# Weight fetches ahead of the modulation pieces, bias rows broadcast in the mixer, one bank waited for per gate product

## What is computed

```python
# first block
mods = silu(c) @ w_ada + b_ada            # 9 pieces of 1024: sh1 sc1 gt1 sh2 sc2 gt2 sh3 sc3 gt3
u = modulate(rmsnorm(h, g_ff1), sh1, sc1)
h = h + 0.5 * gt1 * swiglu(u, w1_gate, w1_up, w1_down)
u = modulate(rmsnorm(h, g_mix), sh2, sc2)
qa, ka, va, xm, o_pre, ga, gb = split(u @ w_in)
ya = diff_attention(qa, ka, va, ...)
xc = silu(causal_conv(xm, conv_w, conv_b))
q, k, v = xc @ w_mq, xc @ w_mk, xm @ w_mv  # per head: the mLSTM's inputs
yb = mlstm(q, k, v, ...)
h = h + gt2 * ((sigmoid(ga) * (ya @ w_proj_a) + sigmoid(gb) * (yb @ w_proj_b)) @ w_out)
u = modulate(rmsnorm(h, g_ff2), sh3, sc3)
h = h + 0.5 * gt3 * swiglu(u, w2_gate, w2_up, w2_down)   # the second feed-forward: "f2"
# second block, twice: shift, scale, gate = silu(c_2) @ ada_w + ada_b ; x = x + gate * layer(...)
# its last layer adds a bias to the scores that depends on the distance: rel_bias[bucket(distance)]
```

## Time and profile before

| | us |
|---|---|
| median of 3 runs | 1200.61 (1199.32 to 1200.76) |
| the profiled execution, device time | 1201.46 |
| its span, first to last instruction | 1199.6 |
| TensorE busy in the span | 1184.5 (99%) |
| VectorE busy | 652.3 (54%) |
| ScalarE busy | 331.9 (28%) |
| GpSimd busy | 82.3 (7%) |
| mean granted TensorE clock | 0.999 of full |

### The profile page before, as it was taken

One profiled execution on the slowest core, in us unless ns is written; L12 is line 12 of the kernel. 1 busy time (PEld: TensorE's weight loads), 2 busy tenths in 40 slices (PEclk: granted clock), 3 DMA queues, 4 the chain that ended last, 5 costly groups with the idle time before them and its releaser, 6 DMA issues.

```text
span 1199.6 us, 19981 instructions
## 1 busy us (share of the span) xinstructions
PE 1184.5 (99%) x8286; PEld 1064.8 (89%) x8286; DVE 652.3 (54%) x1578; ACT 331.9 (28%) x943; POOL 82.3 (7%) x103
## 2 busy tenths in 40 slices
PE   9999999999999999999999999999999999999997
PEld 7889999995778888889999999997888998887887
DVE  4458887280046523351798878657854231167642
ACT  2111210231124434100412120245233431046542
POOL 0000000100011000011000000320003010000111
PEclk9999999999999999999999999999999999999999
DMA  9969949482555455568499967756333643542311
GB/s 346 353 210 307 316 158 308 164 300 72 204 189 183 145 210 210 194 227 293 142 367 323 303 224 230 249 200 222 98 107 141 209 142 113 176 129 83 107 70 36
DMA packets 164138, 241.69 MB, mean 201 GB/s; under 512 B 13921, under 2 KB 112415, under 8 KB 164048
## 3 DMA queue, kind: packets, MB, share of 16 engines
q1 hardware_dynamic: 156160, 230.45, 56.8%
q10 hardware_dynamic: 6784, 5.74, 1.6%
q0 software_dynamic: 1104, 4.22, 1.1%
HBM read 236.82 MB, written 4.62 MB: 201 GB/s over the span
## 4 chain that ended last, share of the span: by engine, by line
PE 91%; DVE 6%; ACT 2%; issue 1%; DMA 1%; POOL 0%; DVEq 0%; ACTq 0%
PE ps L189 88%; DVE arena L198 2%; PE ps L192 2%; DVE tmps L204 1%; DVE arena L207 1%; ACT U L195 1%; ACT tmps L195 1%; DMA bias_row<-rows 0%; DMA arena<-bias_row 0%; DVE rstd L216 0%; DVE tmps L198 0%; ACT arena L195 0%; DVE slots L198 0%; DVE ABT L198 0%; DVE U L198 0%
## 5 line engine op out<-in xcount | busy, mean ns | idle before, releaser
L189 PE MATMUL ps<-U,slots 128*128 128x256 f32 (+2 forms) x2912 | 537.9, 344 | 0.9 <-ACT U L195 0.9
L189 PEld LDWEIGHTS ps<-U,slots 128*128 128x128 f32 (+1 forms) x2912 | 465.5, 190 | 53.2 <-issue 5.0
L189 PE MATMUL ps<-arena,slots 128*128 128x128 f32 (+1 forms) x1840 | 271.1, 308 | 0.0
L189 PEld LDWEIGHTS ps<-arena,slots 128*128 128x128 f32 x1840 | 251.9, 191 | 16.4 <-issue 1.8
L195 ACT ACTIVATE tmps<-ps 128x256 f32<-128x256 f32 (+2 forms) x151 | 57.2, 382 | 345.2 <-PE ps L189 319.6
L207 DVE CUSTOM_DVE_ANT_0 arena<-arena,tmpA 128x1024 f32<-128x1024 f32 x88 | 106.8, 1256 | 14.8 <-DMA arena<-in_w_adaT 14.7
L189 PE MATMUL ps<-arena 128*128 128x128 f32 (+7 forms) x940 | 101.9, 287 | 2.4 <-DVE arena L222 1.5
L189 PEld LDWEIGHTS ps<-arena 128*128 128x128 f32 (+2 forms) x940 | 92.6, 181 | 11.4 <-issue 4.0
L195 ACT ACTIVATE arena<-ps 128x512 f32<-128x512 f32 (+3 forms) x116 | 50.5, 459 | 153.5 <-PE ps L189 149.2
L189 PE MATMUL ps<-ABT,arena 128*128 128x128 f32 (+5 forms) x752 | 81.8, 271 | 0.0
L189 PEld LDWEIGHTS ps<-ABT,arena 128*128 128x128 f32 (+3 forms) x752 | 72.5, 174 | 0.8 <-issue 0.8
(11 more groups left out here) (181 smaller groups left out, 996.6 us busy)
## 6 DMA issues: line engine op xcount, KB each, us to landing
slots<-in_w_in SPq DMA_DIRECT2D x14, 2048.0 KB, 9.3
slots<-in_w_down SPq DMA_DIRECT2D x16, 1408.0 KB, 10.4
slots<-in_w_gate SPq DMA_DIRECT2D x18, 1024.0 KB, 8.2
slots<-in_w_up SPq DMA_DIRECT2D x18, 1024.0 KB, 10.7
arena<-in_w_adaT SPq DMA_DIRECT2D x28, 512.0 KB, 5.9
slots<-in_w_adaT SPq DMA_DIRECT2D x7, 2048.0 KB, 8.1
arena<-in_ada_w1T SPq DMA_DIRECT2D x24, 512.0 KB, 6.3
slots<-in_a_in_w SPq DMA_DIRECT2D x6, 2048.0 KB, 10.4
```

The costliest lines, as they stand in the source:

```text
L189: return Nothing() if self.e is None else self.e.matmul(*a, **k)
```

## The change

It has three parts. In `sync`, block b+2 of the second feed-forward's weights is fetched ahead of the chunks of block b, where before the chunks were fetched first. In `gpsimd`, the 3 MB broadcast of the bias rows moves from behind the squares of n3 to behind the squares of n2, with a new wait in front of it: for TensorE's product of xm pair 1, half 1. In `tensor`, the ring G2 starts at bank 3 instead of bank 0; the first gate product waits for bank 3 alone, and the three others wait each for its own bank, 0, 1 and 2.

```diff
@@ -446,10 +446,10 @@
             fetch("f2 gu", 1)
             e.wait_ge(*pe.at("pb", 3))
             for b in range(11):
+                if b < 9:
+                    fetch("f2 gu", b + 2)
                 for g, c in CHUNKS["f2"].get(b, ()):
                     fetch_chunk(g, c)
-                if b < 9:
-                    fetch("f2 gu", b + 2)
             for p in range(4):
                 fetch("f2 dn", 2 * p)
                 fetch("f2 dn", 2 * p + 1)
@@ -953,7 +953,7 @@
-        G2 = ring(*[b[:, :] for b in banks[0:4]])
+        G2 = ring(*[banks[i][:, :] for i in (3, 0, 1, 2)])
@@ -3078,13 +3078,14 @@
             t_linear(e, "wo", 2, GA, mg, half=1)
             t_sums_half(e, "n3", 0)
             t_linear(e, "wo", 3, GA, mg, half=1)
-            for x in free_of(L) + free_of(S3, 0):
+            for x in free_of(S3, 0):
                 e.wait_ge(*x)
             t_gate(e, "f2", 0, "n3", 0, side=True)
             t_sums_half(e, "n3", 1)
-            t_gate(e, "f2", 1, "n3", 0)
-            t_gate(e, "f2", 0, "n3", 1, side=True)
-            t_gate(e, "f2", 1, "n3", 1)
+            for n, (c, half) in enumerate(((1, 0), (0, 1), (1, 1))):
+                for x in free_of(L, (0, 1, 2)[n]):
+                    e.wait_ge(*x)
+                t_gate(e, "f2", c, "n3", half, side=n == 1)
             for x in free_of(X):
                 e.wait_ge(*x)
             t_gu(e, "f2", 1)
@@ -3743,6 +3744,8 @@
         def gpsimd(e):
             p_bias(e)
             p_squares(e, "n2")
+            e.wait_ge(*pe.at("xm", 1, 1))
+            p_bias_rows(e)
             for pair in range(4):
                 p_rotate(e, "q", pair)
                 p_rotate(e, "k", pair)
@@ -3757,7 +3760,6 @@
             e.wait_ge(*dve.at("mod", 17))
             load_c(e, 1)
             p_squares(e, "n3")
-            p_bias_rows(e)
             p_squares(e, "n4")
```

## The result

The changed kernel takes 1209.38 us (median of 4 runs, 1208.41 to 1210.71), the kernel before beside it 1199.96 (4 runs, 1198.95 to 1200.76): ratio 1.008, 95% interval 1.0062 to 1.0097. The profiled execution has a span of 1208.3 us against 1199.6, a TensorE busy for 1185.1 us (98%) against 1184.5, and a mean granted clock of 0.993 against 0.999.

A forecast was written before the change was run, and what follows sets the result against it. TensorE, busy 1184.5 of 1199.6 us, was taken to bound the kernel. Pause +7.8, clock +2.1, banks -0.57 and weights' order 0 gave +9.3 on 1200.61: about 1210 us; own range 1204.9 to 1214.7, stretched down to 1203 for 8 in 10.

The forecast's parts named there:

- Banks: Second feed-forward's first gate product: 0.86 us pause goes, some 0.5 us comes at the sum of squares; gain 0.57 us.
- Weights ahead of chunks: Second feed-forward: DVE makes the 1.44 us pause without waiting for landings, so earlier weights change 0; bounds -0.5 and +0.5.
- Bias rows: Mixer, first t_ml_qk: bias rows delay w_mk's landing to 273.0, so TensorE stands 7.8 us; bounds 5.7 and 11.2.
- The slack of 1.6 us: Mixer: w_mk lands at 263.6 and TensorE wants it at 265.18, for the first t_ml_qk.
- one window, 551 to 552: Fetch of c_2: q0 had 73.2% and q1 30.1%, taken to show turns by packet, larger packets getting the larger share.
- The work simply adds up: Mixer: w_mk's landing moves by the bias rows' whole 9.45 us of engine work, from 263.6 to 273.0.
- The clock: Behind the pause at the first t_ml_qk: half rate when TensorE goes on, 2.1 us lost; bounds 0 and 2.9.
- my 2.1: Clock loss behind the mixer pause, in us, taken from matmuls at the program's start: 10.40 us against 8.3.
- The 52 instructions at 9.02 us: Program's start: matmul instructions that took 10.40 us against 8.3 at full pace, used to size the clock loss.
- the +0.5: Upper bound for the weights' order: block 2 holds back block 0's chunks until its slot is free.
- The first two: Mixer: bias rows wait for SP's backlog, 1200.0 (chance 0.13); they start late, pause 1 to 4 us, 1201.3 to 1204 (0.07).
- The third: Faster: no clash, late landings hidden in the second feed-forward, so the 1.44 us pause goes; 1198.1, chance 0.02.

The follow-up runs named there:

- The last run: Changed kernel with bias rows issued after w_mk's head 0 product and two of block 1's four chunks moved to blocks 7 and 8: 1198.63 us, 0.9974 of before.
- the 8-row half: Changed kernel with the bias-row broadcast in two DMAs: rows 0 to 7 at the new place, 8 to 15 behind n3's squares: 1207.67 us, ratio 1.0055.
- ACT's queue: Changed kernel with the bias rows issued from ACT, behind its copies of xm pair 1, instead of from POOL: 1207.85 us against 1201.27.

## Why the prediction was right

- **What bounds the kernel.** Right: TensorE's busy time is within 0.6 us the same, and the time moved by TensorE's pauses and its clock alone.
- **Banks.** Right in mechanism and nearly in size: the wait named ACT, was DVE's, went, and part of it came back as POOL's 0.35 us ahead of the sum. -0.57 predicted, -0.49 (changed kernel), -0.50 (alone) measured; the sum takes 0.1 us longer after a pause, which the step left out.
- **Weights ahead of chunks.** 0, and 0.00 measured alone. The last run shows that the 1.44 us pause was DVE's work.
- **Bias rows.** The slack of 1.6 us, the common signal of POOL and SP, the turns of the two queues and the standstill of 7.8 us (8.2 and 7.5 measured, with the restart) all came as worked out. What I took from one window, 551 to 552, carried it. Three steps were cruder than they looked. "The work simply adds up" is true only while the other queue is through first; from ACT's queue it is not, and the pause is 4.9. The work seems to count per engine, not in total, as the 8-row half suggests. And two errors nearly cancel in the 7.8: the broadcast held the engines for 8.7 us beside other traffic (19.8% of 44) instead of the 9.45 that it took alone, but w_mk came 9.8 us later (21.4 for 11.6), 1.1 more than that work. With the bias rows moved alone it is 9.1 for 9.0. What the 1.1 us are, no run takes apart; the engines' share was 0.96 from 264 to 268, so they were not all full to the end.
- **The clock.** Right that it falls and that it costs some us; the size scatters more than I allowed for. The loss in the product behind was 3.15 in the changed kernel, 1.91 with the bias rows alone, 3.08 and 2.75 in the 8-row half and on ACT's queue. My bound of 2.9 was too low, and my 2.1 had a weak source. The 52 instructions at 9.02 us did not come after a time without matmuls, since TensorE had worked from 1.18 us on, and the windows of that profile give a granted clock of 1.00 throughout the first 20 us: that they ran at half clock was concluded from their pace alone. In the profile of the changed kernel the same 52 take 9.79 us, with a granted clock of 0.50 from 8 to 11 us, which by the same sum is a loss of 1.5.
- **The sum.** +9.3 predicted against a median difference of 9.4; on the path it is 10.87 in this profile and 9.37 + (-0.5) = 8.9 when put together from the parts run alone. That the medians agree to 0.1 us is in part luck: one term is a balance of two errors, and another scatters by 1.2 us. The measured 1209.4 lies 0.6 below the forecast because the kernel before took 1199.96 beside it, 0.65 less than the 1200.61 from which I started. The upper end of my range leaves out the +0.5 that I gave the weights' order; nothing hangs on it.
- **The rivals.** The first two fall with the changed kernel's DMA views: from 254 to 255 us, 4.5 us after their issue, the bias rows already had 50.4% of the engines, and from 257 to 258 they had 82.1%. They neither waited for q1's backlog nor started late. The third needed the clash to be absent and landings that hold up DVE; the order of the weights alone moved nothing.

## What to carry to other kernels

A transfer that nobody waits for is not free where it stands: before moving one, look up which awaited transfer is in flight there, how many us lie between its landing and its use, and whether the moved one goes on another queue. On a second queue it took its turns within 5 us of its issue, with a share that was larger with larger packets; behind the awaited one on the same queue, or 17 us later, the same 3 MB cost nothing. And a pause of TensorE in which the clock falls costs more than itself: here 7 to 8 us of standing made 9 to 11.

## What was new about the hardware

The clock was lost in pauses of 4.66, 4.86, 7.33 and 8.04 us and kept in one of 1.76. What it cost afterwards was 1.9 to 3.15 us, in one profile each, and did not follow the length of the pause (3.08 after 4.66, 1.91 after 7.33).

The same broadcast went as packets of 4.6 KB from POOL's queue and of 1.5 KB from ACT's, while the packets were served in nearly equal numbers with those of SP's queue: from 257 to 258 us the bias rows had 82% of the engines' time in the one case and 61% in the other. And a DMA whose outer dimension is 8 was slower for its neighbours than one of the same bytes with 16: w_mk after 18.0 us against 15.1.
